# Key scores and value products of the delta rule moved in among the first attention units

## What is computed

```
# delta rule, 16 heads of 64
state = state * w_t + sa (x) (kk_t * a_t) + v_t (x) k_t      # sa = state . (-kk_t)
y_t   = state . r_t
bonus = sum(r * k * r_k) * v ;  out = (norm(y) * lnx_w + lnx_b + bonus) * g
# attention, 8 heads of 128, two key heads
prob = softmax(q.k / sqrt(128) + bias of the selected keys) ; o = prob . v
```

## Time and profile before

| | us |
|---|---|
| median of three runs | 2552.9 |
| the profiled execution | 2556.89 |
| its span | 2555.1 |
| TensorE matmul busy | 2401.7 (94%) |
| VectorE busy | 1389.0 (54%) |
| ScalarE busy | 1095.4 (43%) |
| the stage around the change (from the first `Aab` product to the `mix` stream) | 1472.0 to 1609.7 |

### The profile page before, as it was taken

The page is one execution under the profiler, slowest core; times in us unless marked ns, Lnnn a source line. Parts: engine busy times, 40 slices in busy tenths (PEclk is TensorE's granted clock), DMA queues, the critical chain, the costliest instruction groups (busy, mean ns, idle before and its releaser), DMA issues.

```text
span 2555.1 us, 29780 instructions
## 1 busy us (share of the span) xinstructions
PE 2401.7 (94%) x12196; PEld 1923.4 (75%) x12196; DVE 1389.0 (54%) x1295; ACT 1095.4 (43%) x1099; POOL 48.5 (2%) x77
## 2 busy tenths in 40 slices
PE   5799999999989899999999779999999999999996
PEld 0487778887568788877887567788888888888885
DVE  0344445547846786566556774655545544545443
ACT  0454545343344444545354633356544334434332
POOL 0100000001000000000000000000000000000000
PEclk7999999999999999999999889999999999999998
DMA  9965455568956696554555001654555565555552
GB/s 390 385 192 163 135 163 180 167 193 327 420 200 213 217 371 214 198 181 157 179 185 175 14 17 31 230 181 150 164 185 186 188 198 182 193 189 189 187 197 98
DMA packets 223185, 497.31 MB, mean 195 GB/s; under 512 B 20825, under 2 KB 22889, under 8 KB 213841
## 3 DMA queue, kind: packets, MB, share of 16 engines
q1 hardware_dynamic: 216528, 458.91, 53.6%
q0 software_dynamic: 6528, 36.56, 3.8%
HBM read 491.77 MB, written 3.67 MB: 194 GB/s over the span
## 4 chain that ended last, share of the span: by engine, by line
PE 63%; DVE 6%; ACT 2%; DMA 2%; issue 1%; DVEq 0%; POOL 0%; ACTq 0%
PE banks L2349 55%; PE banks L2419 2%; DMA raw_eight<-in_w_ada 1%; DVE weights_lo L1396 1%; ACT weights_hi L723 1%; PE banks L2571 1%; PE banks L2608 1%; PE banks L2727 1%; ACT projected L1098 0%; PE banks L2801 0%; PE banks L2554 0%; DVE residual L1756 0%; DVE residual L1761 0%; PE banks L2704 0%; PE banks L2605 0%
## 5 line engine op out<-in xcount | busy, mean ns | idle before, releaser
L1396 DVE TENSOR_TENSOR weights_lo<-weights_raw,weights_hi 128x2048 fp32r<-128x2048 f32 (+1 forms) x356 | 813.5, 2285 | 871.2 <-ACT weights_hi L723 869.4
L723 ACT ACTIVATE weights_hi<-weights_raw 128x2048 fp32r<-128x2048 f32 (+1 forms) x356 | 680.3, 1911 | 1022.3 <-PE banks L2349 989.4
L2349 PE MATMUL banks<-weights_hi,acts_hi 128*128 128x512 f32 (+1 forms) x2240 | 883.8, 395 | 15.8 <-DVE weights_lo L1396 15.3
L2349 PE MATMUL banks<-weights_lo,acts_hi 128*128 128x512 f32 (+1 forms) x2240 | 872.9, 390 | 0.0
L2349 PE MATMUL banks<-weights_hi,acts_lo 128*128 128x512 f32 (+1 forms) x2240 | 872.8, 390 | 0.0
L2349 PEld LDWEIGHTS banks<-weights_hi,acts_hi 128*128 128x128 f32 x2240 | 422.4, 189 | 117.3 <-issue 32.7
L2349 PEld LDWEIGHTS banks<-weights_hi,acts_lo 128*128 128x128 f32 x2240 | 422.2, 188 | 88.0
L2349 PEld LDWEIGHTS banks<-weights_lo,acts_hi 128*128 128x128 f32 x2240 | 422.4, 189 | 85.0 <-issue 1.2
L2349 PE MATMUL banks<-weights_hi,hidden_hi 128*128 128x512 f32 x320 | 125.4, 392 | 0.5 <-DVE weights_lo L1396 0.5
L2349 PE MATMUL banks<-weights_hi,hidden_lo 128*128 128x512 f32 x320 | 124.6, 389 | 0.0
L2349 PE MATMUL banks<-weights_lo,hidden_hi 128*128 128x512 f32 x320 | 124.5, 389 | 0.0
(11 more groups left out here) (507 smaller groups left out, 1929.1 us busy)
## 6 DMA issues: line engine op xcount, KB each, us to landing
weights_raw<-in_w_in_e SPq DMA_DIRECT2D x80, 1024.0 KB, 5.3
raw_eight<-in_w_ada SPq DMA_DIRECT2D x72, 1024.0 KB, 15.3
weights_raw<-in_w_up SPq DMA_DIRECT2D x64, 1024.0 KB, 5.2
weights_raw<-in_w_down SPq DMA_DIRECT2D x64, 1024.0 KB, 5.1
weights_raw<-in_w_in SPq DMA_DIRECT2D x44, 1024.0 KB, 5.0
weights_raw<-in_w_in_o SPq DMA_DIRECT2D x32, 1024.0 KB, 5.6
weights_raw<-in_w_out_e SPq DMA_DIRECT2D x16, 1024.0 KB, 5.1
gate_chunks<-in_w_ada POOLq DMA_DIRECT2D x16, 1024.0 KB, 7.0
```

Of the source, the lines that this page charges most:

```text
L723: eng.activation(WHI[:, c % 2, :, 0:n], RAW[:, sl, :, 0:n], ACT.Copy).then_inc(hi_ready, 1)
L1396: eng.tensor_tensor(WLO[:, c % 2, :, 0:n], RAW[:, c % 4, :, 0:n], WHI[:, c % 2, :, 0:n].bitcast(F32), ALU.subtract).then_inc(lo_ready, 1)
L2349: ins = eng.matmul(BANKS[:, par * 2 + h, 0:s.n], x[:, t, h * P:(h + 1) * P], w[:, c % 2, k, 0:s.n], start=(kc == 0 and k == 0 and m == 0), ...
```

## The change

On TensorE, the four bonus sums now follow `Aab` directly; then the transposed scores `AabT` (in two groups of four jobs, the second called `AabT2`); then the attention units, which take one more step each: `key_values(u-1)` in units 1 to 4, then the key scores `Aak` of k = u in units 0 to 3, or the gate product u-4 in units 4 to 7. The key and b transposes (`keyN`, `bN`) stand behind `Arb` and `Ark`. On VectorE, the bonus products stand ahead of the inverse loop together with the memset of the delta state, and the key-score copies move into the visits of units 2 to 5, which now follow the steps 1, 4, 8, 12, 15, 19, 23, 26 and 30. ScalarE copies the transposed scores, then the attention units with one value-product copy each in units 2 to 5; the copies of `keyN` and `bN` follow the last `Ark` copy, ahead of the activation split of XS. The job list is changed to match.

```diff
@@ job list
-                   ("valN", 4), ("kkb", 4), ("Aab", 8), ("bN", 4), ("AabT", 8)]
-    job_counts += [("Aak0", 2), ("Aak1", 2), ("AKV0", 1), ("Aak2", 2), ("AKV1", 1), ("Aak3", 2), ("AKV2", 1), ("AKV3", 1)]
+                   ("valN", 4), ("kkb", 4), ("Aab", 8)]
+    job_counts += [(f"bonus{j}", 1) for j in range(4)] + [("AabT", 4), ("AabT2", 4)]
+    woven = [[("Aak0", 2)], [("AKV0", 1), ("Aak1", 2)], [("AKV1", 1), ("Aak2", 2)], [("AKV2", 1), ("Aak3", 2)],
+             [("AKV3", 1), ("dgate0", 1)], [("dgate1", 1)], [("dgate2", 1)], [("dgate3", 1)], []]
...
-        if u < 8:
-            job_counts.append((f"bonus{u}" if u < 4 else f"dgate{u - 4}", 1))
-    job_counts += [("keyN", 4), ("Arb", 8), ("Ark", 8), ("cross", 2), ...
+        job_counts += woven[u]
+    job_counts += [("Arb", 8), ("Ark", 8), ("keyN", 4), ("bN", 4), ("cross", 2), ...
@@ ScalarE
-        natural_out("bN", BN)
-        for j in range(8):
-            jj = J["AabT"] + j
...
+        transposed_out(0)
+        transposed_out(1)
...
+            if 2 <= u <= 5:
+                key_values_out(u - 2)
             if 6 <= u <= 9:
                 tiles_out(f"dgate{u - 6}", GT, f0=2 * (u - 6))
-        natural_out("keyN", KN)
...
         copied(eng, J["Ark"] + 7)
+        natural_out("keyN", KN)
+        natural_out("bN", BN)
         for q in (2, 3):
             split_hi(XS, q)
@@ VectorE
-        eng.wait_ge(S("score_zeroed"), 4)
-        for k in range(4):
+        def key_scores(k):
+            if k == 0:
+                eng.wait_ge(S("score_zeroed"), 4)
...
+        UNIT_AT = (1, 4, 8, 12, 15, 19, 23, 26, 30)
+        def unit_step(u):
+            if u < 8:
+                dsa_max(u)
+            if u >= 1:
+                dsa_recip(u - 1)
+            if 2 <= u <= 5:
+                key_scores(u - 2)
+        for j in range(4):
+            bonus(j)
+        eng.wait_ge(S("a_ab_stored"), 64)
         flat_t = TC[:, :, :].rearrange("p a b -> p (a b)")
         ch.link(eng.memset(flat_t, 0.0))
         ch.link(eng.memset(flat_t[:, 0:C * C:C + 1], 1.0))
+        ch.link(eng.memset(ST[:, :, :], 0.0))
+        eng.wait_ge(S("a_by_chunk_in"), 16)
...
-            if t >= 4 and t % 3 == 1:
...
+            if t in UNIT_AT:
+                unit_step(UNIT_AT.index(t))
@@ TensorE
         chunk_matrices(pairs_of("Aab"), KK, AT)
-        token_jobs("bN", AT)
-        chunk_matrices(pairs_of("AabT"), AT, KK)
...
+        def woven_step(u):
+            if 1 <= u <= 4:
+                key_values(u - 1)
+            if u < 4:
+                key_scores(u)
+            elif u < 8:
+                gate_product(u - 4)
+        for j in range(4):
+            bonus_sums(j)
+        transposed_scores(0)
+        transposed_scores(1)
...
-            if u < 8:
-                (bonus_sums if u < 4 else gate_product)(u % 4)
-        token_jobs("keyN", KTR)
+            woven_step(u)
...
+        token_jobs("keyN", KTR)
+        token_jobs("bN", AT)
```

More of the change, by code:

```diff
@@ L400, in build @@
             job_counts.append((f"dsa_o{u - 1}", 1))
-        if u < 8:
-            job_counts.append((f"bonus{u}" if u < 4 else f"dgate{u - 4}", 1))
-    job_counts += [("keyN", 4), ("Arb", 8), ("Ark", 8), ("cross", 2), ("corner", 2), ("R0", 2), ("U0", 2), ("S", 2), ("R1", 2), ("U1", 2)]
+        job_counts += woven[u]
+    job_counts += [("Arb", 8), ("Ark", 8), ("keyN", 4), ("bN", 4), ("cross", 2), ("corner", 2), ("R0", 2), ("U0", 2), ("S", 2), ("R1", 2), ("U1", 2)]
     job_counts += [("ycent", 4), ("yvar", 1), ("ybc", 4), ("memT", 8), ("x3T", 8), ("ckT", 2), ("cqT", 2)]
@@ L1195, in _, with transposed_out, key_values_out @@
         ch.done("decays")
-        natural_out("bN", BN)
-        for j in range(8):
-            jj = J["AabT"] + j
[L1199 to L1202, removed]
-        for k in range(4):
+        def transposed_out(half):
+            for j in range(4):
+                jj = J[("AabT", "AabT2")[half]] + j
+                u = half * 16 + j % 2 * 8 + 4 * (j // 2)
+                bank_full(eng, jj)
+                free(eng.activation(AABT[:, u:u + 4, :].rearrange("p a b -> p (a b)"), bank(jj), ACT.Copy), jj)
+        def key_values_out(k):
             jj = J[f"AKV{k}"]
@@ L2127, in dsa_recip @@
             ch.done("dsa_recip")
-        eng.wait_ge(S("a_by_chunk_in"), 16)
+        UNIT_AT = (1, 4, 8, 12, 15, 19, 23, 26, 30)
[9 more added lines that the diff above has]
+        eng.wait_ge(S("a_ab_stored"), 64)
         flat_t = TC[:, :, :].rearrange("p a b -> p (a b)")
@@ L2138, in _ @@
             ch.link(eng.tensor_tensor(TC[:, 0:s, t + 1:C], TC[:, 0:s, t + 1:C], prod, ALU.add))
-            if t >= 4 and t % 3 == 1:
-                u = (t - 4) // 3
-                if u < 8:
[L2142 to L2146, removed]
+            if t in UNIT_AT:
+                unit_step(UNIT_AT.index(t))
         ch.done("inverse_ready")
@@ L2149, in _ @@
         ch.done("inverse_ready")
-        eng.wait_ge(S("a_ab_stored"), 64)
-        ch.link(eng.memset(ST[:, :, :], 0.0))
         for j in range(8):
@@ L2809, in _ @@
         chunk_matrices(pairs_of("Aab"), KK, AT)
-        token_jobs("bN", AT)
-        chunk_matrices(pairs_of("AabT"), AT, KK)
-        eng.wait_ge(S("scaled"), 1)
         def key_values(k):
@@ L2828, in key_values, with key_scores, transposed_scores @@
             eng.sem_inc(S("key_scores_used"), 1)
[L2830 to L2834, removed]
+        def key_scores(k):
+            eng.wait_ge(S("scaled"), 1)
+            chunk_matrices([(k, (J[f"Aak{k}"], J[f"Aak{k}"] + 1))], KTR, KK)
+        def transposed_scores(half):
+            j0 = J[("AabT", "AabT2")[half]]
+            chunk_matrices([(2 * half + i, (j0 + 2 * i, j0 + 2 * i + 1)) for i in range(2)], AT, KK)
+        def woven_step(u):
[5 more added lines that the diff above has]
+                gate_product(u - 4)
+        for j in range(4):
+            bonus_sums(j)
+        transposed_scores(0)
+        transposed_scores(1)
         eng.wait_ge(S("att_values_kept"), 1)
```

## The result

The changed kernel takes 2565.43 us (median of 17 runs, 2563.01 to 2577.27) against 2553.37 for the kernel before in the same series (17 runs, 2550.43 to 2562.24): ratio 1.0041, 95% interval 1.0031 to 1.0051. That is 10.5 us slower by the ratio, 7.9 to 13.0 by its interval (12.1 between the medians); 2562 was predicted. The profiled execution took 2565.78, span 2564.0.

The account below looks back on a forecast made before the run. TensorE held 63% of the chain; the touched stretch was bound by VectorE's inverse loop, then TensorE. Cross products +8.0 and corner products +1.0 gave +9.0 us: 2565.9 against the profiled execution, 2562 for a median, range 2547 to 2572.

Parts of the forecast that it names:

- The path before the loop: Ahead of the attention units: first score 12.6 us earlier, VectorE's inverse loop starting 9.6 us earlier.
- the mechanism in the loop: Inverse loop: four rotating side banks make VectorE wait for key-score pairs whose banks its own maximum has just started to release.
- The three visits: VectorE's visits 3, 4 and 5 in the loop: idle ahead of key-score copies, 10.7 to 13.4 us together, taken as 12.
- The round trip: In the loop, from VectorE's maximum through ScalarE's exponentials and copy to TensorE's key-score pair: 5.0 to 6.0 us.
- That rival: ScalarE's value-product copy holds the next exponentials, each of three or four visits up to 2 us later; +16, 2569; chance 0.20.
- The wait for score 7: VectorE's visit 7, score 7 queued behind the first gate product: wait 2.3 to 3.2 us, taken as 2.7, before 1.5.
- the last output: TensorE behind the loop, running without a gap from score 7: last output ends at 1558.2 instead of 1552.1, +6.1 us.
- the loop's end: VectorE's inverse loop ends at 1550.3, 5.1 us later than before.
- The corner products: Behind the cross products, waiting for ScalarE's cross copy, late through transpose copies and activation split: about +1.0 us (0 to 1.5).
- The cross products: Behind the loop, after the moved key and b transposes: start at 1577.0 instead of 1569.0, +8.0 us.
- Weaving pays: Rival: banks come free in time, loop ends 8.2 us earlier, in all -4, so 2549; chance 0.17.
- Half waits: Rival: only the score's bank is late, each wait about 1.5 us shorter, sum +3 to +5, 2557; chance 0.13.

Follow-up runs that it names:

- e5: Changed kernel with ScalarE's copy of each value product one unit later; 2567.67 us, ratio 1.0055 to the kernel before.
- e1: Changed kernel with key scores and value products in PSUM banks 0 to 3 instead of the four shared side banks; 2552.19 us, ratio 0.9987 to the kernel before.
- unwoven: Changed kernel with key scores and value products back ahead of the attention units; 2561.03 us, ratio 1.0021 to the kernel before; profiled again at 2557.59.
- e4: e1 plus b transposes and first gate product in unit 0, other gates one unit earlier, key transposes between r-score pairs; 2549.56 us, ratio 0.9976 to kernel before.
- e7: Changed kernel with b and key transposes and their copies back in their old places (old tail); 2571.66 us, ratio 1.0055 to kernel before; second profile 2561.99.
- e2: Changed kernel with the key-score pair first in its unit, ahead of score u+2, same four banks; 2579.84 us, ratio 1.0083 to the kernel before.
- e6: Changed kernel with the four gate products one unit later (units 5 to 8); 2564.85 us, ratio 1.0045 to the kernel before.
- e8: e4 with gate products 1 and 2 ahead of the probabilities in units 2 and 3, in own banks; 2553.02 us, ratio 0.9998 to the kernel before.

## Why the prediction was right

**Where the cost is.** The path before the loop (first score -12.6, measured -12.8; loop start -9.6, measured -9.3) and the mechanism in the loop came as worked out. The three visits were to wait 12 us together, and waited 13.1. The round trip of 5.0 to 6.0 took 6.06 in the first of them: exponentials, scaling and copy took exactly the 2.57 from the earlier trace rows, and the excess is the value copy, which put the start of the exponentials 1.72 behind the maximum instead of 1.05. That rival was right in kind and small in size, 1.0 us by e5. That the rotation, and not the added work, is the cause is shown by e1.

**The terms that were too small.** The wait for score 7 was set at 2.7 and came out at 4.4. Of its parts the exponentials (1.74 against 1.6) and the gate product (2.78 against 2.4) held; the score itself was taken from the row before at the full clock, 2.0, and took 3.5 from 1542.06 to the maximum's start, at a granted 0.51. I had allowed for the half clock in the pairs and not in this score. The loop thus ended 6.9 late instead of 5.1, and the last output 8.0 instead of 6.1. Loop start, copies' waits and this last wait were together 3.1 too small; that the loop's end was off by only 1.8 is luck in part, since the work between the waits took 41.1 us where the sum has 42.3. The corner products were set at +1.0 and came at +1.8 (4.3 behind the cross products, 2.5 before). Here the prediction's sum was wrong in itself: its own terms, 1.5 to the split, 2.23 for it and 0.6 for the copy, give 4.3 and not 3.5 to 3.9, and 4.3 less 2.5 is the 1.8 that came. The parts came otherwise (0.97, 2.30, 0.39 of idle time, 0.60), with the same total. The cross products (+8.0, measured +9.8) only carry the loop's error. The stage became 11.7 longer, not 9.0; with 2552.9 as the start that is 2564.6, near the 2565.43 measured. The size of the change was thus put too low, 9 against 10.5 (by the ratio) to 12.1 (by the medians), and its cause rightly.

**The shares.** With the second profiles, all of one chip, the parts can be told apart: unwoven 139.5, changed kernel 144.9, old tail 142.2, kernel before (its first profile) 133.4. The weaving costs 5.4 and the moved transposes 2.7. The remaining 3.4 or so come with the rest, the bonus in front and the gate in the last units: without the weaving, the loop starts 2.6 later than before and its last maximum waits 4.4 too (1.5 before), behind the gate product of 4.51 us at half clock. These are differences between single executions, good to a microsecond or two, and the last of them lies across chips.

**The rivals.** Weaving pays holds only with banks of its own: in e1 the loop ends earlier than before (70.7 against 73.2), and the time is 8.8 us under the unwoven kernel's of the same series. Against the kernel before, e1 alone does not show a gain (its interval reaches 1.0000); e4 does. The rule on interleaving, Perfetto Trace Analysis, section Optimization Strategy, of the Trainium skill, spoke for that rival; the trace is against it for the change as made (+0.41%) and allows it where the interleaved jobs bring their own banks (e4: -0.24%). Half waits falls: all three pairs were released by the probabilities' bank, none by the score's alone.

**What stays open.** Why the clock falls in one execution and not in another of the same kernel, in the same place, and what in e4 could prevent it. The second profiles of the unwoven kernel and of the one with the old tail were taken on another chip than the first; that the nine times of e7, on one chip, fall in two groups speaks for the execution, and does not settle it.

## What to carry to other kernels

When jobs share banks in a fixed rotation, write beside each new job whose reader must release its bank, and whether that reader stands, in its own order, behind this very job: a consumer that wants a job whose bank depends on work that it has just released waits a whole round trip, each time. Moving such a job forward only passes the wait to whoever is queued behind it (e2); other banks remove it (e1). And work put into another engine's waits is worth what it takes off the end of the chain there: a place where the last consumer is early, as VectorE is behind the loop (e6), gives nothing back.

## What the runs showed of the hardware

I had not expected that two executions of one program can differ by several microseconds through the clock of a few small products. The same solve ran at a granted 0.50 in one execution and 0.94 in another, 4.4 us apart, and the same front of the unwoven kernel at 0.50 and 1.00, 6.5 us apart at the first score. The half clock set in behind waits of 3.24 us, and in e1 behind one of 1.96. It also set in without such a wait: in the first execution of the unwoven kernel it fell from 1.00 to 0.50 between 1493 and 1494, among the key scores and value products, where the longest wait of TensorE in the 14 us before was 0.52 us. The Trainium skill, TensorE: Matmul & The Clock Gate, section HAM oscillation, describes such bursts between waits that each start cold; the traces agree in kind, e.g. 3.51 instead of 1.90 for a value product in e1. With an effect of 12 us in 2550, a single profile can lie further from its kernel's median than what it is to show (5.5 us in e4, 8.8 in e8, 9.7 in the second of e7), so the series of times and second profiles had to decide.
